# Rotary halves swapped by two rounded products, cosine products ahead of the swap

## The reference, cut to what matters

```
qh = (rms_norm_2(c_q, g_q) @ w_uq).reshape(B, S, 8, 128 + 64)
q_nope = qh[..., :128]
q_rope = apply_rope(qh[..., 128:], cos, sin)
kv = (rms_norm_2(c_kv, g_kv) @ w_ukv).reshape(B, S, 8, 128 + 128)
k_nope, v = kv[..., :128], kv[..., 128:]
k_rope = apply_rope(k_r, cos, sin)
s = einsum(q_nope, k_nope) + einsum(q_rope, k_rope)

def apply_rope(x, cos, sin):
    x1, x2 = x[..., :half], x[..., half:]
    return concatenate([x1 * cos - x2 * sin, x1 * sin + x2 * cos])
```

## Time and profile before

| | us |
|---|---|
| median of three executions | 830.85 |
| lowest, highest | 830.24, 831.02 |
| the profiled execution | 829.83 |
| its span in the trace | 828.0 |
| TensorE busy in the span | 818.8 |
| VectorE busy in the span | 564.3 |
| ScalarE busy in the span | 496.3 |

### The profile page before, as it was taken

One profiled execution on the slowest core, in us unless ns is written; L12 is line 12 of the kernel. 1 busy time (PEld: TensorE's weight loads), 2 busy tenths in 40 slices (PEclk: granted clock), 3 DMA queues, 4 the chain that ended last, 5 costly groups with the idle time before them and its releaser, 6 DMA issues.

```text
span 828.0 us, 13533 instructions
## 1 busy us (share of the span) xinstructions
PE 818.8 (99%) x5160; PEld 717.9 (87%) x5160; DVE 564.3 (68%) x1051; ACT 496.3 (60%) x859; POOL 21.1 (3%) x27
## 2 busy tenths in 40 slices
PE   8999999999999999999999999999999999999997
PEld 7998998989888888888878789878888889999785
DVE  6443447876977777785886766379776575669765
ACT  6655457774576565665575335677685574665554
POOL 0000000004400000000000000000000001000000
PEclk9999999999999999999999999999999999999999
DMA  9765752235535555546535444434444645445312
GB/s 345 289 214 219 263 196 103 103 107 207 194 137 192 191 203 180 180 177 225 184 122 204 152 143 163 153 132 173 153 153 169 235 154 193 164 153 203 108 46 76
DMA packets 21835, 144.05 MB, mean 174 GB/s; under 512 B 2545, under 2 KB 3185, under 8 KB 5136
## 3 DMA queue, kind: packets, MB, share of 16 engines
q1 hardware_dynamic: 20880, 140.50, 47.9%
q10 hardware_dynamic: 896, 2.73, 1.0%
HBM read 142.17 MB, written 1.05 MB: 173 GB/s over the span
## 4 chain that ended last, share of the span: by engine, by line
PE 97%; ACT 1%; DMA 1%; DVE 0%; issue 0%; DVEq 0%; SPq 0%
PE PS L526 95%; DMA xa<-x 1%; PE PS L779 1%; PE PS L1479 0%; ACT PB L1766 0%; PE PS L1012 0%; PE PS L1013 0%; PE PS L1014 0%; PE PS L1295 0%; PE PS L1318 0%; PE PS L1345 0%; ACT PB L1603 0%; ACT hx L1583 0%; DVE xb L2812 0%; ACT PB L1609 0%
## 5 line engine op out<-in xcount | busy, mean ns | idle before, releaser
L2209 DVE TENSOR_TENSOR wl<-ring,wh 128x1024 fp32r<-128x1024 f32 x248 | 305.2, 1236 | 184.6 <-ACT wh L1569 181.9
L1569 ACT ACTIVATE wh<-ring 128x1024 fp32r<-128x1024 f32 x247 | 260.1, 1058 | 199.5 <-PE PS L526 181.0
L526 PE MATMUL PS<-hx,wh 128*128 128x256 f32 (+1 forms) x1832 | 352.6, 306 | 0.1
L526 PEld LDWEIGHTS PS<-hx,wh 128*128 128x128 f32 x1832 | 288.8, 191 | 15.7 <-issue 3.9
L526 PE MATMUL PS<-wh,hx 128*128 128x512 f32 (+1 forms) x896 | 248.4, 394 | 0.5 <-ACT hx L1583 0.5
L526 PE MATMUL PS<-hx,wl 128*128 128x256 f32 x1084 | 246.7, 283 | 0.0
L526 PEld LDWEIGHTS PS<-wh,hx 128*128 128x128 f32 x896 | 166.0, 188 | 36.8 <-issue 3.0
L526 PEld LDWEIGHTS PS<-hx,wl 128*128 128x128 f32 x1084 | 184.1, 191 | 3.4
L526 PE MATMUL PS<-wl,hx 128*128 128x512 f32 (+1 forms) x448 | 138.4, 388 | 0.0
L526 PEld LDWEIGHTS PS<-wl,hx 128*128 128x128 f32 x448 | 83.7, 188 | 17.3 <-DVE wl L2209 0.2
L1886 ACT ACTIVATE T<-PS 128x512 f32<-128x512 f32 x22 | 13.2, 599 | 27.4 <-PE PS L526 27.4
(11 more groups left out here) (318 smaller groups left out, 680.0 us busy)
## 6 DMA issues: line engine op xcount, KB each, us to landing
ring<-w SPq DMA_DIRECT2D x127, 1024.0 KB, 4.8
cn<-consts SPq DMA_DIRECT2D x2, 1051.0 KB, 10.8
V<-gains ACTq DMA_DIRECT2D x3, 512.0 KB, 4.4
cn<-consts SPq DMA_DIRECT2D x1, 1050.5 KB, 8.5
xa<-x SPq DMA_DIRECT2D x2, 512.0 KB, 4.6
out<-xb SPq DMA_DIRECT2D x4, 256.0 KB, 2.0
ring<-w SPq DMA_DIRECT2D x2, 256.0 KB, 4.9
ring<-w SPq DMA_DIRECT2D x1, 512.0 KB, 7.0
```

The costliest lines, as they stand in the source:

```text
L526: return nc.tensor.matmul(o, lhsT, rhs, start=start, stop=stop, skip_group_check=True)
L1569: A(wh[:, q % SPLITS, :], ring[:, i % RING, e:e + HALF], ACT.Copy).then_inc(sem("hi_ready"), 1)
L2209: TTn(wl[:, q % SPLITS, :], ring[:, PLACE[unit_of(q)] % RING, e:e + HALF], wh[:, q % SPLITS, :].bitcast(F32), ALU.subtract).then_inc(sem(" ...
```

## The change

The swaps become pairs of float32r products. ACT copies `rope_swap` once to a rounded tile (`swap_hi`, in the tile `er`), and rounds each source to a high part in `wsx` (`rope_high`). DVE subtracts to get the low part (`rope_low`) and writes it over tiles 1 and 2 of `hl`. TensorE then multiplies `swap_hi` by the high and by the low part. Since the matrix holds only 0, 1 and -1, it needs no low part itself. Swap 0 moves from behind bank 5 to behind bank 6. `rotate` loses its cosine product, which becomes `turned_by` and stands ahead of the swap's result on DVE; the rest of `rotate(0)` moves from bank 5's turn to the start of bank 7's.

```
+        swap_hi, rope_lo = er[:, 0:P], hx[:, 1:3, 1, :]
+        rope_parts = ((wsx[:, 0:512], rope_lo), (wsx[:, 0:512], rope_lo), (wsx[:, 512:768], hl[:, 1, :]))
 TensorE
-                pe.wait_ge(*((sem(f"uq_read[{n}]"), 3) if n < 2 else read(FIRST["lora"] + 2)))
+                pe.wait_ge(sem("lora_ready"), 6 + n)
                 if n >= 1:
                     pe.wait_ge(sem("rope_swapped_read"), n)
-                mm(PS[:, SC[1], 0:w_], c("rope_swap"), src, True, True).then_inc(sem("rope_swapped"), 1)
+                mm(PS[:, SC[1], 0:w_], swap_hi, hi, True, False)
+                mm(PS[:, SC[1], 0:w_], swap_hi, lo, False, True).then_inc(sem("rope_swapped"), 1)
...
-            rope_swap(0, QR[:, 0:2, :])
...
+                if n == 6:
+                    rope_swap(0)
+            rope_swap(1)
...
 ScalarE
+            def rope_high(n, src):
+                A(rope_parts[n][0], src, ACT.Copy).then_inc(sem("rope_tables"), 1)
+            act.wait_ge(sem("late_in"), 32)
+            A(swap_hi, c("rope_swap"), ACT.Copy).then_inc(sem("rope_tables"), 1)
+            rope_high(2, KR[:, 0, :])
             for n in range(0, 14, 2):
...
+                if n == 4:
+                    act.wait_ge(sem("uq_read[0]"), 3)
+                    rope_high(0, QR[:, 0:2, :])
...
+                if n == 6:
+                    act.wait_ge(sem("uq_read[1]"), 3)
+                    act.wait_ge(sem("rope_swapped"), 1)
+                    rope_high(1, QR[:, 2:4, :])
 VectorE
+            def rope_low(n, src):
+                hi, lo = rope_parts[n]
+                dve.wait_ge(sem("rope_tables"), (5, 6, 4)[n])
+                if n:
+                    dve.wait_ge(sem("rope_swapped"), n)
+                TTn(lo, src, cols2(hi.bitcast(F32)) if n < 2 else hi.bitcast(F32), ALU.subtract)\
+                    .then_inc(sem("lora_ready"), 1)
...
             for n in range(1, 14, 2):
+                if n == 7:
+                    halves(UQ_HALF[n] + SPLITS)
+                    rotate(0, QR[:, 0:2, :])
...
                 if n == 5:
-                    rotate(0, QR[:, 0:2, :])
+                    rope_low(0, QR[:, 0:2, :])
+                    turned_by(0, QR[:, 0:2, :])
+                if n == 7:
+                    rope_low(1, QR[:, 2:4, :])
+                    turned_by(1, QR[:, 2:4, :])
...
                 if n == 9:
                     halves(UQ_HALF[n] + SPLITS + 1)
                     rotate(1, QR[:, 2:4, :])
+                    rope_low(2, KR[:, 0, :])
...
                 if n == 11:
+                    turned_by(2, KR[:, :, :])
                     rotate(2, KR[:, :, :])
```

More of the change, by code:

```diff
@@ L1384, in _, with rope_swap @@
             pe.wait_ge(sem("lora_rs"), 1)
-            def rope_swap(n, src):
-                pe.wait_ge(*((sem(f"uq_read[{n}]"), 3) if n < 2 else read(FIRST["lora"] + 2)))
+            def rope_swap(n):
+                pe.wait_ge(sem("lora_ready"), 6 + n)
                 if n >= 1:
                     pe.wait_ge(sem("rope_swapped_read"), n)
+                hi, lo = rope_parts[n]
                 w_ = 512 if n < 2 else 256
-                mm(PS[:, SC[1], 0:w_], c("rope_swap"), src, True, True).then_inc(sem("rope_swapped"), 1)
+                mm(PS[:, SC[1], 0:w_], swap_hi, hi, True, False)
+                mm(PS[:, SC[1], 0:w_], swap_hi, lo, False, True).then_inc(sem("rope_swapped"), 1)
             def uq_bank(n):
@@ L1424, in _ @@
                 m.then_inc(sem(UQ_DONE[n][0]), 1)
-            rope_swap(1, QR[:, 2:4, :])
+                if n == 6:
+                    rope_swap(0)
+            rope_swap(1)
             for half in range(2):
@@ L1452, in _ @@
                 if n == 11:
-                    rope_swap(2, KR[:, 0, :])
+                    rope_swap(2)
             def mla_scores(p):
@@ L2871, in _, with turned_by @@
             z_gated(5)
-            def rotate(n, src):
+            def rope_low(n, src):
+                hi, lo = rope_parts[n]
+                dve.wait_ge(sem("rope_tables"), (5, 6, 4)[n])
[3 more added lines that the diff above has]
+                    .then_inc(sem("lora_ready"), 1)
+            def turned_by(n, src):
                 tiles = 2 if n < 2 else 1
                 dve.wait_ge(sem("rope_tables"), 2)
[L2875 to L2878, removed]
+                a = T2[:, 0, 0:tiles * S]
                 if n:
@@ L2881, in rotate @@
                 own(TTn(cols2(a, tiles), src, ropes[0].unsqueeze(1).broadcast_to([P, tiles, S]), ALU.mult))
+            def rotate(n, src):
+                tiles = 2 if n < 2 else 1
+                a, b = T2[:, 0, 0:tiles * S], T2[:, 1, 0:tiles * S]
+                dve.wait_ge(sem("rope_swapped"), n + 1)
                 TTn(cols2(b, tiles), cols2(PS[:, SC[1], 0:tiles * S], tiles),
```

## The result

The changed kernel has a median of 833.90 us over six executions, from 832.42 to 834.70; the kernel before, over six, 830.49 (830.24 to 831.02). The ratio is 1.004, 95% interval 1.003 to 1.005. It is 3.4 us slower; 833.6 was predicted.

The account below looks back on a forecast made before the run. TensorE, busy 99% of the span and 97% of the chain, was taken as the bound. Waits of 2.65 and 1.1 us less 0.99 saved give +2.76; 830.85 + 2.76 = 833.6 us, range 832.0 to 835.4.

Parts of the forecast that it names:

- The saving: TensorE's three swaps as float32r pairs: 0.40 + 0.40 + 0.19 = 0.99 us saved, entirely on the path.
- Swap 0 waits for the chain over half 8: Behind bank 6, TensorE waits for `rope_low(0)`, behind bank 5's copy and half 8's split: 2.65 us idle, bounds 2.15 to 3.1.
- the hand-over to TensorE: From the end of `rope_low(0)` to swap 0's start: some 0.15 us for the wait and weight load.
- Swap 1 waits for the chain over half 9: Behind bank 9, TensorE waits for `rope_low(1)`, behind bank 7's copy and half 9's split: 1.1 us idle, bounds 0.8 to 1.5.
- The forecast's case: Both swaps 0 and 1 wait and the clock stays up: 2.65 + 1.1 - 0.99 = +2.76 us, chance 0.60.
- rival 1: Clock halves in swap 0's new idle, costing 1.1 to 2.2 us more after give-back at swap 1: say 835.2 us, chance 0.20.
- The base: Starting time for the forecast: the kernel before at 830.85 us, its median, 1.02 above the profiled execution.
- the short chains: Lower end of the forecast range, 832.0 us, said to be reached if the chains to swaps 0 and 1 are short.
- What was to cost nothing: Rounded matrix and `rope_high(2)` in ACT's 1.25 us idle, swap 2, third sum, cosine order and DMA waits: no added time.

Follow-up runs that it names:

- e4: Changed kernel with its new order, but each swap one float32 product straight from the source, no high or low parts: 830.18 us, against 830.22 for the kernel before.
- e1: Changed kernel with both low parts made earlier on DVE, that of swap 0 in a place of its own: 829.11 us, against 830.22 for the kernel before.
- e2: Changed kernel with only swap 0's low part made early, swap 1's left behind bank 7's copy: 830.72 us, against 830.22 for the kernel before.
- e3: Changed kernel plus five unused float32 products of 256 columns in the idle ahead of swap 0: 832.52 us, against 830.22 for the kernel before.
- e5: Changed kernel run again without edit, for its spread: 833.89 us, against 830.19 for the kernel before.
- e6: Changed kernel with rotation 0's cosine product put ahead of its low part on DVE, lengthening swap 0's wait: 834.27 us, against 830.19 for the kernel before.
- e8: Changed kernel with swap 0 behind bank 8 and swap 1 behind the first w_fd half on TensorE: 829.84 us, against 830.19 for the kernel before.
- e7: Changed kernel plus two unused float32 products of 256 columns in the idle ahead of swap 0: 832.55 us, against 830.19 for the kernel before.

## Why the prediction was right or wrong

**The saving.** 0.99 us predicted, 1.07 measured by time between e4 and e1. The rows of e1 give 0.83: from the end of bank 5 (749.73 - 1.44 = 748.29) to the scores it takes 766.63 - 748.29 = 18.34 us, against 19.17 before. In the rows of the changed kernel swap 2 takes 0.23 and swap 1 takes 0.56 in place of 0.46: the first product behind an idle has a distance of 0.33 us to the next, not 0.23. The same 0.10 is in e2, and in e1 at swap 1 (754.59 to 754.93), where the gap ahead is 0.08 us. This 0.10 and the gap are, but for rounding, what e1's rows are short of 0.99.

**Swap 0 waits for the chain over half 8.** Right in place and releaser, link by link. The idle is 2.47 us, not 2.65. From the end of bank 5 to the end of the low part it was to be 751.93 - 748.01 = 3.92 us; it was 751.57 - 747.70 = 3.87 (bank 6's twelve products, 1.44 us before 749.14, start at 747.70). Of the 0.18 too much, 0.05 lie in this chain and 0.13 in the hand-over to TensorE, which was taken as 0.15 and rounded up, and is 0.04 in the chain after.

**Swap 1 waits for the chain over half 9.** Right, 1.03 us against 1.1. From bank 7's last product to DVE's slot for the low part, 3.29 us were forecast, and 758.11 - 754.82 = 3.29 measured. That this wait depended on the first was not seen; e2 shows 1.83 for it alone. The prediction took what DVE does between banks 5 and 7 as hidden, which holds only while TensorE idles first.

**The two waits together.** With the clock up they cost 832.52 - 829.11 = 3.4 us by time (e3 against e1; both have the cheap products), 0.3 less than the 3.75 of the forecast. The forecast's case, both waits with the clock staying, was priced at +2.76. It is the kernel e3, whose 832.36 to 832.87 us lie with the lower group's 832.42 to 832.90. It measured 832.52 - 830.22 = +2.3 by time, and +2.68 by rows from the end of bank 5 to the scores (769.87 - 748.02 = 21.85 us against 19.17): waits of 2.46 and 1.01 us, 0.10 for the first product behind each, less the 0.99. So this case was understood; it was not the usual one.

**The clock.** This was rival 1, at 0.20, and the step that failed is the weight against it: that neither wait stands alone and TensorE is full before and between them. The clock fell all the same, in both profiled executions of the changed kernel, and by time and mean clock in eight of eleven. So the case that the forecast called likeliest is the rarer one. The earlier trace rows had shown a fall 2.1 us after the last product; in the changed kernel it came after 1.9 and 2.1. Its price was given as 1.1 to 2.2 us, with part given back at swap 1. Measured: swap 0 and bank 7 take 754.95 - 751.61 = 3.34 us, against 2.01 with the clock up (e3), which is 1.33 lost, and 1.41 in e5. Nothing was given back in these two, for the clock was whole before bank 8, and the chain for swap 1 starts only at the end of bank 7. In e6, where the fall came later, 0.45 us were given back, by the mechanism that the rival named. Against 832.52 the median is 1.4 higher. The Trainium skill ("TensorE: Matmul & The Clock Gate", Part 1) says that the halved clock is the default and that activity releases it. The trace of the changed kernel agrees: the clock fell in the 2.47 us idle, and it was whole again at 754.6, with TensorE at work since 751.61.

**The number.** 833.6 us was met by luck. The forecast was 830.85 + 3.75 - 0.99. The base, a median of three executions, was high: six give 830.49, and the 48 beside the experiments 830.2. Split by medians, the time is 830.22 + 3.41 - 1.07 + 1.37 = 833.93 us, the last term being the clock, 833.89 - 832.52. The clock's term had been left out, and a base 0.6 too high, waits 0.3 too large and a saving 0.1 too small made up for most of it. The rows are a check of their own: the two waits, the two slower first products, the saving and the clock give 2.47 + 1.03 + 0.20 - 0.99 + 1.33 = +4.04 us, and from the end of bank 5 to the scores it is 770.90 - 747.70 - 19.17 = +4.03. The two profiled executions are only 3.77 us apart, since the changed kernel's reached the end of bank 5 0.31 us sooner. What the base can't hide is the difference: +2.76 was forecast and +3.4 measured, +3.7 beside the experiments. The range had a slip too: its lower end of 832.0 was called the short chains, but their bounds add up to 830.85 + 2.15 + 0.8 - 0.99 = 832.8.

**What was to cost nothing.** e4 shows this for the order of the rotation to within its interval, and e1 for the work added on ACT and DVE, as no wait is left there. In the changed kernel `rope_high(1)` waited 2.69 us on ACT and delayed nothing, as ACT's next split still waited 1.65 us for bank 7 (its timeline):

```profile
752.93 0.63 ACT L2134 ACTIVATE wsx<-QK 128x512 fp32r<-128x512 f32 x1 [2.69 <-PE PS L528]
755.21 1.06 ACT L1574 ACTIVATE wh<-ring 128x1024 fp32r<-128x1024 f32 x1 [1.65 <-PE PS L528]
```

**What stays open.** Whether the lower group's executions had no fall at all, or a shorter one, rests on times and mean clocks alone, since none of them was profiled. That is also open for the 833.30 of e6. What decides between the groups was not found. Nor was it tried why the upper group spreads over 1.2 us; of the 0.49 us between its two profiled executions, 0.43 lie ahead of the end of bank 6 (749.14 and 749.57), before the first wait.

## What to carry to other kernels

A cheaper operation whose operands need preparing is worth what it saves only if the preparation is done before the bottleneck asks for it. Here it was not, since it stood on its engine behind work that itself waits for the bottleneck. Moving it ahead of that work (e1) removed both waits and kept the gain; moving the swaps back on TensorE (e8) removed them too, but made the scores wait. Follow each new wait to the last thing in the queue before it, and compare that chain with the work that covers it: here 3.9 us against 1.44 and 2.88. When TensorE must idle as long as here (2.47 us), add the clock's fall to the price, and fill the idle if it can't be removed: two throw-away products, which left 1.6 us of it, did as much as five.

## What the runs showed that was not expected

- An idle of 1.6 us left the clock at full, and so did 1.8 us (e7 and e2, one profiled execution each; the narrow ranges of all eight and all eleven say the same). 2.47 us brought it to half in both profiled executions, and by time and mean clock in eight of eleven.
- The fall can come behind the idle: in e6 0.7 us after TensorE had started again. It then reached into banks that work while the next wait's chain runs, and part of its price was given back.
- Removing one of two waits can lengthen the other: 1.03 us became 1.83.
- Five products whose results nobody reads, 2.15 us of them, made the kernel 1.4 us faster.
